# First attention: the rotation's swap of rows by small on-chip DMA transfers in place of matmuls

## The reference

```python
def apply_partial_rope(t, cos, sin):
    ...
    r1, r2, rest = t[..., :half], t[..., half:ROT_DIM], t[..., ROT_DIM:]
    return jnp.concatenate([r1 * c - r2 * s, r1 * s + r2 * c, rest], axis=-1)

def diff_attention(x, w_qkv, w_o, lq1, lk1, lq2, lk2, sub_g, lambda_init, cos, sin):
    qkv = x @ w_qkv
    q, k, v = jnp.split(qkv, [QK_WIDTH, 2 * QK_WIDTH], axis=-1)
    q = apply_partial_rope(q.reshape(B, S, N_HEADS, 2, HEAD_DIM), cos, sin)
    k = apply_partial_rope(k.reshape(B, S, N_HEADS, 2, HEAD_DIM), cos, sin)
    ...
        p = jax.nn.softmax(jnp.where(mask, s, -jnp.inf), axis=-1)
        a = (p[:, :, 0] - lam * p[:, :, 1]).astype(v.dtype)
        outs.append(jnp.einsum('bhqk,bhkd->bhqd', a, vb))
```

## Time and profile before

| | |
|---|---|
| median of 3 runs | 2112.25 us (2106.28 to 2113.55) |
| the profiled execution | 2108.74 us, span 2106.7 us |
| TensorE (PE) busy | 1988.1 us, 94% of the span |
| VectorE (DVE) busy | 694.7 us, 33% |
| ScalarE (ACT) busy | 403.8 us, 19% |
| GpSimd (POOL) busy | 117.2 us, 6% |
| mean granted clock of TensorE | 0.982 |

### The profile page before, as it was taken

How to read it: one execution, slowest core, us unless ns; L and a number is a source line. 1 busy time by engine, 2 the same in 40 slices (tenths; PEclk the granted TensorE clock), 3 DMA queues, 4 the chain that set the end, 5 groups by cost and what they waited for, 6 DMA issues and landing times.

```text
span 2106.7 us, 25585 instructions
## 1 busy us (share of the span) xinstructions
PE 1988.1 (94%) x10125; PEld 1062.1 (50%) x10125; DVE 694.7 (33%) x1670; ACT 403.8 (19%) x874; POOL 117.2 (6%) x140
## 2 busy tenths in 40 slices
PE   8999989999999999899999999999699999999787
PEld 4444446545454544745645454544454445665454
DVE  0155557221111111735321111112638233632124
ACT  1133432111111111111111111111224322122112
POOL 0000001000000000000100000000010001111100
PEclk9999998999999999999999999999899999999999
DMA  9611104899999999922799999999931111699995
GB/s 336 201 40 40 41 20 143 349 419 420 420 420 421 420 420 380 332 69 80 294 420 419 420 421 420 421 420 418 337 114 40 40 40 44 229 372 420 419 419 209
DMA packets 123826, 595.59 MB, mean 283 GB/s; under 512 B 15751, under 2 KB 43287, under 8 KB 60767
## 3 DMA queue, kind: packets, MB, share of 16 engines
q1 hardware_dynamic: 110559, 568.06, 67.9%
q0 software_dynamic: 13184, 26.40, 3.7%
HBM read 572.95 MB, written 37.01 MB: 290 GB/s over the span
## 4 chain that ended last, share of the span: by engine, by line
PE 80%; DMA 13%; DVE 3%; ACT 1%; issue 1%; SPq 0%; another core or an unknown queue 0%; DVEq 0%; ACTq 0%
PE bank L998 21%; PE bank L657 10%; PE bank L1041 10%; PE bank L914 10%; DMA ring<-in_moe_w_up_dram 8%; PE bank L810 5%; DMA ring<-in_w_up_dram 5%; PE bank L671 4%; PE bank L643 3%; PE bank L1172 1%; PE bank L760 1%; PE bank L733 1%; PE bank L905 1%; PE bank L1133 1%; PE bank L720 1%
## 5 line engine op out<-in xcount | busy, mean ns | idle before, releaser
L998 PE MATMUL bank<-ring,work 128*64 128x512 f32 (+1 forms) x3008 | 563.2, 526 | 27.4 <-DMA ring<-in_w_up_dram 22.6
L998 PEld LDWEIGHTS bank<-ring,work 128*64 128x64 f32 x3008 | 225.0, 138 | 361.4 <-issue 333.1
L1041 PE MATMUL bank<-ring,work 128*64 128x512 f32 x1280 | 295.8, 600 | 3.9 <-DVE work L1869 3.9
L1869 DVE COPY work<-bank 128x256 f32<-128x256 f32 (+1 forms) x96 | 36.5, 380 | 693.0 <-PE bank L906 693.0
L914 PE MATMUL bank<-work 128*128 128x128 f32 x2112 | 253.3, 278 | 0.0
L914 PEld LDWEIGHTS bank<-work 128*128 128x128 f32 x2112 | 240.8, 192 | 6.3 <-issue 2.0
L657 PE MATMUL bank<-hT,ring 128*128 128x512 f32 x512 | 234.9, 600 | 0.7 <-ACT work L1235 0.7
L1329 ACT ACTIVATE work<-bank 64x512 f32<-64x512 f32 x96 | 56.6, 589 | 547.2 <-PE bank L1041 544.6
L1041 PEld LDWEIGHTS bank<-ring,work 128*64 128x64 f32 x1280 | 84.3, 136 | 143.9 <-issue 129.1
L657 PEld LDWEIGHTS bank<-hT,ring 128*128 128x128 f32 x512 | 92.7, 191 | 105.2 <-issue 103.3
L1317 ACT ACTIVATE work<-bank 64x512 f32<-64x512 f32 (+1 forms) x96 | 49.7, 518 | 475.1 <-PE bank L998 475.1
(11 more groups left out here) (308 smaller groups left out, 1669.8 us busy)
## 6 DMA issues: line engine op xcount, KB each, us to landing
ring<-in_moe_w_down_dram SPq DMA_DIRECT2D x128, 1024.0 KB, 17.5
ring<-in_moe_w_gate_dram SPq DMA_DIRECT2D x126, 1024.0 KB, 16.4
ring<-in_moe_w_up_dram SPq DMA_DIRECT2D x126, 1024.0 KB, 18.3
ring<-in_w_down_dram SPq DMA_DIRECT2D x32, 1024.0 KB, 25.4
ring<-in_w_gate_dram SPq DMA_DIRECT2D x31, 1024.0 KB, 23.2
ring<-in_w_up_dram SPq DMA_DIRECT2D x31, 1024.0 KB, 24.5
ring<-in_attn_w_qkv_dram SPq DMA_DIRECT2D x12, 1024.0 KB, 12.3
work<-y_rows SPq DMA_DIRECT2D x12, 1024.0 KB, 7.0
```

The lines of the kernel that those rows point to most:

```text
L998: mm = pe.matmul(GU2[s % 2][BLK * a:BLK * a + BLK, 0:F], xgT[pair % 2][:, per * kk + k, BLK * of_pair:BLK * of_pair + BLK], v[a][:, k, :], ...
L1041: mm = pe.matmul(DN[BLK * n:BLK * n + BLK, :], hT_[:, 2 * kk + k, :], v[:, k, 512 * n:512 * n + 512], start=(kk + k == 0), stop=(2 * kk + ...
```

## The change

The matmul `permute` is taken out. Four DMA transfers per chunk, issued on POOL's queue, copy 8 rows each from `raw` into `swapped`, a new tile of 128x512 that is cleared once at the start. VectorE's rotation reads `swapped` in place of the bank. It moves from step 2cc+2 to step 2cc+3. TensorE may write a bank again as soon as ScalarE has copied it to `raw`; ScalarE waits for the rotation two chunks back before it writes `raw` again. POOL waits for `raw` of the chunk and for the rotation of the chunk before.

```diff
-            def permute(cc):
-                pe.wait_ge(at.raw, cc + 1)
-                pe.matmul(bank[cc % 2][:, :], rope_p, raw[cc % 2], start=True, stop=True).then_inc(at.perm, 1)
...
-                    pe.wait_ge(at.rope, 15 + i)
+                    pe.wait_ge(at.raw, 15 + i)
...
                         if cc >= 2:
-                            pe.wait_ge(at.rope, cc - 1)
+                            pe.wait_ge(at.raw, cc - 1)
...
-                if st % 2 == 0 and 1 <= 4 * pair + st // 2 <= 16:
-                    permute(4 * pair + st // 2 - 1)
...
                     wait_half(act, first["qk"] + 2 * pair + n // 2, n % 2)
+                    if cc >= 2:
+                        act.wait_ge(at.rope, cc - 1)
                     act.activation(raw[cc % 2], bank[cc % 2][:, :], ACT.Copy, scale=-0.125 if n < 2 else 1.0)\
...
+            dve.memset(swapped, 0.0)
             dve.memset(zeros[:, :], 0.0).then_inc(zero_ready, 1)
...
             def rope(cc):
-                dve.wait_ge(at.perm, cc + 1)
+                dve.wait_ge(at.perm, 64 * (cc + 1))
...
-                dve.tensor_tensor(rtmp, bank[cc % 2][:, :], ropes, ALU.mult)
+                dve.tensor_tensor(rtmp, swapped, ropes, ALU.mult)
...
-                if step % 2 == 0 and 1 <= step // 2 <= 16:
-                    rope(step // 2 - 1)
+                if step % 2 == 1 and 0 <= (step - 3) // 2 < 16:
+                    rope((step - 3) // 2)
...
+            pool.wait_ge(zero_ready, 1)
+            for cc in range(16):
+                pool.wait_ge(at.raw, cc + 1)
+                if cc:
+                    pool.wait_ge(at.rope, cc)
+                for lo in (0, 8, 64, 72):
+                    pool.dma_start(swapped[lo:lo + 8, :], raw[cc % 2][lo ^ 8:(lo ^ 8) + 8, :]).then_inc(at.perm, 16)
             load_norm(0, 0, at.negmax, 64)
```

More of the change, by code:

```diff
@@ L108, in program @@
         ident, tri, ones = con[:, C_ID:C_ID + P], con[:, C_TRI:C_TRI + P], con[:, C_ONE:C_ONE + P]
-        causal, rope_p = con[:, C_CAUS:C_CAUS + P], con[:, C_ROPE:C_ROPE + P]
+        causal = con[:, C_CAUS:C_CAUS + P]
         h = sb("h", [P, T, D])
@@ L425, in program @@
         raw = [wk(14848 + 512 * i, 512) for i in range(2)]
-        rtmp = wk(15872, 512)
+        rtmp, swapped = wk(15872, 512), wk(17920, 512)
         ropec, ropes = wk(16384, 512), wk(16896, 512)
```

## The result

| | before | changed |
|---|---|---|
| median of the runs, 4 each | 2112.9 us (2106.28 to 2114.79) | 2096.54 us (2091.96 to 2097.72) |
| the profiled execution | 2108.74 us, span 2106.7 | 2091.96 us, span 2090.1 |

The ratio is 0.992, 95% interval 0.9902 to 0.9938: the changed kernel is 16.4 us faster by the medians, and 13 to 21 by the interval. The forecast was 2099.0 us with 2091 to 2107, a gain of 13.3.

What follows compares the result with a forecast made beforehand. TensorE, nearly gapless in attention, was taken as the bound. Removed permutes of 14.3 us less a 1.0 us stall gave 13.3 us, moving the median from 2112.25 to 2099.0 us, range 2091 to 2107 for 8 in 10.

Steps and rivals of the forecast that it cites:

- The rows of permutes: TensorE in attention: 16 permutes removed, three at 0.86 us and thirteen at 0.90, saving 14.3 us, bounds 13.8 and 15.1.
- The swaps: POOL's four transfers per chunk: 4.5 us calm, 7.7 us loaded, from ScalarE's `raw` to landing.
- The ring: Swap and rotation wait for each other over one `swapped`: one turn takes 6.5 us calm, 9.8 us loaded.
- stall 1.0 us: First pair: TensorE waits before `scores(0)` for rotation 2, worked out as 0.9 us, taken as 1.0.
- the bound of 7.5 us: Upper bound of TensorE's wait before `scores(0)`, if every swap takes 6.5 us to land.
- VectorE's rotation in odd steps: Attention's wide steps: rotation between maxima and combine delays `a` to 176.3, TensorE wants it at 176.8; slack 0.4 us, cost nothing.
- POOL's issuing against VectorE: Attention: whether POOL's transfer issues slow VectorE's operations and eat the 0.4 us slack; the earlier trace showed no slowing.
- Rival 2: Six wide attention steps: POOL issues hold VectorE's tensor_scalar, `a` late, costing 1 to 5 us; about 2102 us, chance 0.09.
- The rest is shifted along: Behind attention: later stages, including the big DMA stream, move forward with TensorE, so attention's gain carries whole to the end.
- Rival 3: Attention throughout: the ring becomes the bound once landing exceeds 8.2 us; at 10 us some 28 us slower, 2140; chance 0.06.
- Rival 4: Behind attention: lower-clock stretches of TensorE fall otherwise after the shift and give gain back; 2106 to 2112 us, chance 0.11.

Runs made afterwards that it cites:

- doubled permute: The kernel before with each of the 16 permute matmuls issued twice into the same bank: 2127.62 us against 2111.45, ratio 1.008.
- both executions of the changed kernel: The profiled execution of the first comparison, 2091.96 us, and one of the unmodified changed kernel measured again later: median 2099.82 us against 2115.15, ratio 0.9938.
- sister kernel: The changed kernel with VectorE's rotation in the even step 2cc+2 behind combine, TensorE's order untouched: 2099.99 us, ratio 0.9937.
- turn-first kernels: The changed kernel with TensorE's turn (transposes) of `a` ahead of `scores`: 2089.34 us; the same with VectorE's rotation back in even steps: 2088.82 us.
- the run with sixteen transfers: The changed kernel with sixteen transfers per chunk in place of four, the added ones copying rows whose sine is zero: 2144.67 us against 2111.29.

## Why the prediction was right, point by point

*The rows of permutes.* Three at 0.86 us in the first pair: `scores(0)` comes 2.58 us sooner (26.50 to 23.92). Thirteen later: the remainder, 201.64 to 189.79, is 11.85 us, 0.91 each, where 0.90 was taken of 0.86 to 0.96. Sum 14.43 against 14.3. The doubled permute gives the same price from the other side.

*The swaps.* The ring was put at 6.5 us calm; it is 6.0 to 6.2. The median from issue to landing of the 64 transfers is 1.8 us, below the 2.8 taken:

```profile
work<-work POOLq DMA_DIRECT2D x64, 16.0 KB, 1.8
```

What I left out, 0.6 us from the end of `raw` or of a rotation to POOL's first issue (78.99 to 79.59), made up for half of it. The term "stall 1.0 us" was mis-sized: it is 0 in both executions of the changed kernel. But the room was not the same in both: rotation 2 ended 1.9 us before `scores(0)` in the first (100.44 against 102.31) and only 0.4 us in the second (101.41 against 101.79), where swap 1 had taken longer to land. So the zero was in part luck, and the bound of 7.5 us was not idle: one execution of a sister kernel had 4.0 us of wait and 1.7 of lower clock.

By the rule of the Trainium skill that the prediction cited ("DMA: Bandwidth & Descriptors", section "Anatomy of one DMA — SWDGE (gpsimd) path": 2.0 us fixed) the stall would be nothing. Where the traffic is light the trace agrees, with 1.8 us; under load it does not, with up to 5.0 us from issue to landing.

*VectorE's rotation in odd steps.* `a` was to be done at 176.3 with 0.4 us of slack. In the changed kernel scores of the wide step start at 164.98 and `a` is done 6.24 us later; the next scores start at 171.46. It holds, and TensorE never waits for it. Taking the slack away, as the turn-first kernels do, raises the waits for `a` from 2.1 us to 9.8: it was as thin as stated.

*POOL's issuing against VectorE.* tensor_scalar at 169.95 lasts 0.48 us while POOL issues from 170.07 on. In the kernel before, in the same step of the earlier trace rows, it is

```profile
173.84 0.49 DVE L1565 TENSOR_SCALAR work<-work,small 128x512 f32<-128x512 f32 x1
```

The four issues take 2.06 us beside it and 2.08 with VectorE idle (79.59). It is no single case: five of the changed kernel's eight tensor_scalars of this width overlap an issue, and their mean is 486 ns, against 487 for the other three; none of the 64 issues takes more than 0.55 us. Rival 2 has no ground here. The rule of the Trainium skill, "SBUF — State Buffer", section "Who interferes with whom", would have one of the two stand still for the whole of the other's instruction; no row here shows it.

*The rest is shifted along.* The part behind attention varies by 10.7 us between executions (1798.0 to 1808.7, leaving out the kernel without the swaps), so one execution can't show that the shift is whole; the medians do, with 16.4 and 15.3 us for 14.4 of attention, and 16.2 for the 13.7 of the doubled permute. Rival 3 is real but far: it takes a ring of some 12 us, and then costs more than I had worked out. Rival 4's variation exists, and between the two executions of the changed kernel it is the clock, as the rival had it (0.983 and 0.980 over the span); but it is not tied to the change.

The total was forecast 13.3 and is 14.4 in the stretch, 15 to 16 in the medians. The step that did the work, matmuls off a gapless engine, was right and sized to 0.1 us; the 1.1 us between are, but for 0.1, the stall that did not come.

## What to carry to other kernels

If the trace shows an engine without gaps, an operation taken from its order is worth its place in the stream (0.86 to 0.91 us here, not the 1.02 to 1.12 us that its row lasts), and the work may go to a much slower path, so long as that path's whole turn (issue, landing, consumer, hand-back) is shorter than the period at which the pieces come. Check the shortest period and the busiest moment, not the mean, and look at more than one execution: the room before the wait was 1.9 us in one and 0.4 in the next. And once the bound engine is shorter, look at what stands ahead of the chain it waits for: moving a rotation nobody needed yet from ahead of combine to behind it, together with the turn, gave 17 us more, while the move of the turn alone gave 8.

## What the runs showed of the hardware that I had not expected

A stall of TensorE cost more than its length: after 5.8 us of standing still the granted clock was 0.50 for 3 us (1.4 us lost), after 4.0 us some 1.7 us were lost, and after 17.5 us eight matmuls took 5.99 in place of 3.60 us. Where waits kept coming, in the run with sixteen transfers, the lower clock made the same matmuls 14.1 us longer, as much as the waits themselves behind `scores(0)` (14.5).

Transfers of 16 KB from SBUF to SBUF, issued on POOL's queue, landed 1.8 us after their issue in calm, and up to 5.0 us after it when a single 1 MB load had been issued on another queue shortly before.

Executions of the same code differed in two places. Behind attention it was the granted clock (0.983 and 0.980 over the span, 7 us). In the first 75 us the first copy came between 75.0 and 78.4 us: in the changed kernel the first eight matmuls of TensorE's chain add 6.45 us to it, in the kernel before 3.70; what set this is not known.
